# Attention values computed with the probabilities as the stationary operand, and normalised before they are turned

## The reference

```python
s = einsum('bqhd,bkhd->bhqk', q, k) * 64 ** -0.5 + bias      # causal, dilated, selected or decayed
p = softmax(s, axis=-1)
o = einsum('bhqk,bkhd->bqhd', p, v)                           # then concatenated, @ w_out
```

## Time and profile before

| | before |
|---|---|
| median of 3 runs | 2513.5 us (2513.25 to 2513.96) |
| the profiled execution | 2513.96 us |
| its span | 2512.2 us |
| TensorE busy | 2414.5 us, 96% |
| VectorE busy | 1071.5 us, 43% |
| ScalarE busy | 952.6 us, 38% |
| GpSimd busy | 1006.1 us, 40% |
| mean granted TensorE clock | 0.983 |

### The profile page before, as it was taken

How to read it: one execution, slowest core, us unless ns; L and a number is a source line. 1 busy time by engine, 2 the same in 40 slices (tenths; PEclk the granted TensorE clock), 3 DMA queues, 4 the chain that set the end, 5 groups by cost and what they waited for, 6 DMA issues and landing times.

```text
span 2512.2 us, 29431 instructions
## 1 busy us (share of the span) xinstructions
PE 2414.5 (96%) x11844; PEld 1936.9 (77%) x11844; DVE 1071.5 (43%) x1947; ACT 952.6 (38%) x1322; POOL 1006.1 (40%) x789
## 2 busy tenths in 40 slices
PE   7999999999999989999999988999999998999997
PEld 6777588888877766888888757888888867888886
DVE  4677541221347765221226465422225757422224
ACT  5345352332443444322335444422223484422222
POOL 4423054444443232444445413344444333444442
PEclk9999999999999999999999989999999999999998
DMA  4212022322232121322322211233322312223331
GB/s 150 84 51 93 17 85 100 101 92 93 83 103 84 51 76 34 101 91 94 101 101 97 84 34 51 84 101 101 97 89 84 118 50 77 88 89 101 101 101 51
DMA packets 138279, 212.36 MB, mean 85 GB/s; under 512 B 7456, under 2 KB 65952, under 8 KB 137888
## 3 DMA queue, kind: packets, MB, share of 16 engines
q1 hardware_dynamic: 138144, 210.48, 25.9%
HBM read 208.36 MB, written 2.10 MB: 84 GB/s over the span
## 4 chain that ended last, share of the span: by engine, by line
PE 54%; DVE 5%; ACT 2%; issue 2%; POOL 1%; POOLq 0%; DVEq 0%; ACTq 0%
PE ps L306 45%; PE ps L331 4%; DVE x L653 1%; POOL w_lo L269 1%; PE ps L1696 1%; PE ps L468 1%; PE ps L771 1%; PE ps L752 1%; PE ps L792 1%; DVE h_lo L543 0%; DVE tmp_both L648 0%; ACT w_hi L260 0%; PE ps L1191 0%; PE ps L1199 0%; DVE p_more L457 0%
## 5 line engine op out<-in xcount | busy, mean ns | idle before, releaser
L269 POOL TENSOR_TENSOR w_lo<-raw,w_hi 128x512 fp32r<-128x512 f32 (+1 forms) x776 | 995.6, 1315 | 1470.0 <-ACT w_hi L260 1470.0
L306 PE MATMUL ps<-h_hi,w_hi 128*128 128x512 f32 x1696 | 681.1, 402 | 12.7 <-POOL w_lo L269 10.8
L306 PE MATMUL ps<-h_hi,w_lo 128*128 128x512 f32 x1696 | 662.8, 391 | 0.0
L306 PE MATMUL ps<-h_lo,w_hi 128*128 128x512 f32 x1696 | 662.7, 391 | 0.0
L260 ACT ACTIVATE w_hi<-raw 128x2048 fp32r<-128x2048 f32 (+2 forms) x196 | 363.4, 1855 | 743.4 <-PE ps L306 725.0
L306 PE MATMUL ps<-hid_hi,w_hi 128*128 128x512 f32 x992 | 390.4, 394 | 5.0 <-DVE hid_lo L861 3.9
L306 PEld LDWEIGHTS ps<-h_hi,w_hi 128*128 128x128 f32 x1696 | 319.4, 188 | 88.7 <-issue 21.3
L306 PE MATMUL ps<-hid_hi,w_lo 128*128 128x512 f32 x992 | 387.2, 390 | 0.0
L306 PE MATMUL ps<-hid_lo,w_hi 128*128 128x512 f32 x992 | 387.0, 390 | 0.0
L306 PEld LDWEIGHTS ps<-h_lo,w_hi 128*128 128x128 f32 x1696 | 319.3, 188 | 69.1 <-issue 5.8
L306 PEld LDWEIGHTS ps<-h_hi,w_lo 128*128 128x128 f32 x1696 | 318.8, 188 | 68.9 <-issue 0.6
(11 more groups left out here) (292 smaller groups left out, 2810.1 us busy)
## 6 DMA issues: line engine op xcount, KB each, us to landing
raw<-in_w_up SPq DMA_DIRECT2D x32, 1024.0 KB, 5.2
raw<-in_w_down SPq DMA_DIRECT2D x32, 1024.0 KB, 5.0
raw<-in_ffn_w_gate SPq DMA_DIRECT2D x44, 512.0 KB, 4.0
raw<-in_ffn_w_up SPq DMA_DIRECT2D x44, 512.0 KB, 5.0
raw<-in_w_in SPq DMA_DIRECT2D x20, 1024.0 KB, 5.0
raw<-in_ffn_w_down SPq DMA_DIRECT2D x20, 1024.0 KB, 5.1
raw<-in_w_out SPq DMA_DIRECT2D x8, 1024.0 KB, 5.1
raw<-in_ev_w_in SPq DMA_DIRECT2D x8, 1024.0 KB, 5.3
```

Of the source, the lines that this page charges most:

```text
L269: pool.tensor_tensor(w_lo[r][:, k, 0:slot.width], raw[r][:, k, 0:slot.width], w_hi[r][:, k, 0:slot.width].bitcast(F32), ALU.subtract).then ...
L306: mm = pe.matmul(o, lh, rh, start=first and q == 0, stop=last and q == 2, skip_group_check=True)
```

## The change

`values` runs for one unit at a time, with the turned probabilities (128 columns) stationary and the values (64 columns) moving. The result is token-major, one head beside the other, in bank 3. VectorE inverts the row sums and multiplies them in by broadcast, from bank 3 into `on` (in the place of `rb`). TensorE turns the normalised result in `back`, four transposes into bank 2, and the high and the low part are made from there. `rb`, its turning and its copy are gone. The order in TensorE's step becomes scores, turn, beside, values, back, and VectorE's product moves to the step 4 behind the last unit, high and low part to the step 6 behind it.

```diff
@@ values, turn_sums
+            def values(self, pe, i):
+                j, qb, e = self.units[i]
+                h, c = 2 * j + e, (2 * qb + e) * HD
+                pe.wait_ge(*at("pT_copied", self.u0 + i + 1))
+                if i % 8 == 0 and j >= 1:
+                    pe.wait_ge(*at("o_norm", self.b0 + j))
                 for kb in range(qb + 1):
-                    for e in range(2):
-                        h = 2 * j + e
-                        mm = pe.matmul(ps[HD * e:HD * e + HD, 3, qb * P:(qb + 1) * P],
-                                       self.v[:, kb, h * HD:(h + 1) * HD], pT[(i + e) % self.TS][:, kb, :],
-                                       start=kb == 0, stop=kb == qb, skip_group_check=True)
+                    mm = pe.matmul(ps[:, 3, c:c + HD], pT[i % self.TS][:, kb, :],
+                                   self.v[:, kb, h * HD:(h + 1) * HD], start=kb == 0, stop=kb == qb,
+                                   skip_group_check=True)
                 sg["pv_done"].by(mm)
+
+            def back(self, pe, j, turned):
+                pe.wait_ge(*at("o_norm", self.b0 + j + 1))
+                pe.wait_ge(*at("pT_copied", self.u0 + turned))
+                for qb in range(TB):
+                    mm = pe.transpose(ps[:, 2, qb * P:(qb + 1) * P],
+                                      on[:, 2 * qb:2 * qb + 2, :].rearrange("p a b -> p (a b)"), ident)
+                sg["oT_ready"].by(mm)
+                self.backs += 1
@@ turn
-                if self.turned:
-                    pe.wait_ge(*at("rb_copied", self.b0 + self.turned))
+                if self.backs:
+                    pe.wait_ge(*at("mix_lo", self.b0 + self.backs))
@@ tensor
-                    u = i - self.VAL - 1
-                    if 0 <= u < n and u % 2 == 0:
-                        self.values(pe, u)
-                    j = self.at_end(i, self.TURN_SUMS)
-                    if j is not None:
-                        self.turn_sums(pe, j)
-                        beside(i)
                     if self.TURN <= i < n + self.TURN:
                         self.turn(pe, i - self.TURN)
-                    if j is None:
-                        beside(i)
+                    beside(i)
+                    if self.VAL <= i < n + self.VAL:
+                        self.values(pe, i - self.VAL)
+                    j = self.at_end(i, self.VAL + 2)
+                    if j is not None:
+                        self.back(pe, j, min(n, i - self.TURN + 1))
@@ vector
-                    j = self.at_end(i, self.SUMS)
+                    j = self.at_end(i, self.VAL)
                     if j is not None:
-                        dve.wait_ge(*at("p_ready", self.u0 + 8 * j + 8))
-                        link(dve, dve.reciprocal(sr[:, 8 * j:8 * j + 8], sd[:, 8 * j:8 * j + 8]))
-                        if self.b0 + j:
-                            dve.wait_ge(*at("o_norm", self.b0 + j))
-                        sg["sr_ready"].by(dve.tensor_copy(
-                            rb[:].rearrange("p (h d) -> p h d", d=HD),
-                            sr[:, 8 * j:8 * j + 8].unsqueeze(2).to_broadcast([P, 8, HD])))
-                    j = self.at_end(i, self.OUT)
-                    if j is not None:
-                        dve.wait_ge(*at("rb_copied", self.b0 + j + 1))
-                        dve.wait_ge(*at("pv_done", (self.u0 + 8 * j + 8) // 2))
-                        sg["o_norm"].by(dve.tensor_tensor(self.key[:, self.mix0 + j, :], ps[:, 3, :], rb[:], ALU.mult))
-                    j = self.at_end(i, self.LOW)
+                        dve.wait_ge(*at("pv_done", self.u0 + 8 * j + 8))
+                        if j >= 1:
+                            dve.wait_ge(*at("oT_ready", self.b0 + j))
+                        a0, a1 = 8 * j, 8 * j + 8
+                        link(dve, dve.reciprocal(sr[:, a0:a1], sd[:, a0:a1]))
+                        sg["o_norm"].by(dve.tensor_tensor(
+                            on[:], ps[:, 3, :].rearrange("p (h d) -> p h d", d=HD),
+                            sr[:, a0:a1].unsqueeze(2).to_broadcast([P, 8, HD]), ALU.mult))
+                    j = self.at_end(i, self.VAL + 2)
                     if j is not None:
                         dve.wait_ge(*at("mix_hi", self.b0 + j + 1))
                         b = self.mix0 + j
-                        sg["mix_lo"].by(dve.tensor_tensor(hid_lo[:, b, :], self.key[:, b, :],
-                                                          hid_hi[:, b, :].bitcast(F32), ALU.subtract))
+                        sg["mix_lo"].by(dve.tensor_tensor(hid_lo[:, b, :], ps[:, 2, :], hid_hi[:, b, :].bitcast(F32),
+                                                          ALU.subtract))
@@ scalar
-                    j = self.at_end(i, self.TURN_SUMS)
-                    if j is not None:
-                        act.wait_ge(*at("rb_ready", self.b0 + j + 1))
-                        sg["rb_copied"].by(act.activation(rb[:], ps[:, 2, :], ACT.Copy))
...
-                            act.wait_ge(*at("pv_done", (u - self.TS) // 2 + 1))
+                            act.wait_ge(*at("pv_done", u - self.TS + 1))
...
-                    j = self.at_end(i, self.HIGH)
+                    j = self.at_end(i, self.VAL + 2)
                     if j is not None:
-                        act.wait_ge(*at("o_norm", self.b0 + j + 1))
-                        sg["mix_hi"].by(act.activation(hid_hi[:, self.mix0 + j, :], self.key[:, self.mix0 + j, :],
-                                                       ACT.Copy))
+                        act.wait_ge(*at("oT_ready", self.b0 + j + 1))
+                        sg["mix_hi"].by(act.activation(hid_hi[:, self.mix0 + j, :], ps[:, 2, :], ACT.Copy))
```

More of the change, by code:

```diff
@@ L148, in build @@
         stat = place("stat", [P, 4 * P])
-        rb = place("rb", [P, S], where=t_off["rs2"])
+        on = place("on", [P, 8, HD], where=t_off["rs2"])
         colT = place("colT", [P, TB * IDX_H + 2 * TB])
@@ L171, in build @@
             "pool_hi pool_lo gn_in gn_mean gn_c gn_sq gn_var gn_rstd gn_out ret_hi ret_lo mix_hi mix_lo s_ready "
-            "s_masked nmax p_ready pT_ready pT_copied pv_done sr_ready rb_ready rb_copied o_norm post xup wf_split x_final stored "
+            "s_masked nmax p_ready pT_ready pT_copied pv_done o_norm oT_ready post xup wf_split x_final stored "
             "f_mm f_in f_c f_done pool_in pool_mm pool_out bias_ready conv_done xi_done root_done lru_mm lru_r lru_t "
@@ L734, in build, with __init__ @@
             TURN, VAL = 2, 4
-            SUMS, TURN_SUMS, OUT, HIGH, LOW = 2, 3, 5, 6, 7
-            def __init__(self, heads, q_hi, q_lo, val, key, bias, mix0, u0, b0, decay=None):
-                self.q_hi, self.q_lo, self.v, self.key, self.bias = q_hi, q_lo, val, key, bias
+            def __init__(self, heads, q_hi, q_lo, val, bias, mix0, u0, b0, decay=None):
+                self.q_hi, self.q_lo, self.v, self.bias = q_hi, q_lo, val, bias
                 self.mix0, self.u0, self.b0, self.decay = mix0, u0, b0, decay
@@ L773, in turn @@
                 sg["pT_ready"].by(mm)
[L775 to L781, removed]
             def values(self, pe, i):
-                j, qb, _ = self.units[i]
-                pe.wait_ge(*at("pT_copied", self.u0 + i + 2))
-                if i % 8 == 0 and self.b0 + j:
+                j, qb, e = self.units[i]
+                h, c = 2 * j + e, (2 * qb + e) * HD
+                pe.wait_ge(*at("pT_copied", self.u0 + i + 1))
+                if i % 8 == 0 and j >= 1:
                     pe.wait_ge(*at("o_norm", self.b0 + j))
                 for kb in range(qb + 1):
-                    for e in range(2):
-                        h = 2 * j + e
-                        mm = pe.matmul(ps[HD * e:HD * e + HD, 3, qb * P:(qb + 1) * P],
-                                       self.v[:, kb, h * HD:(h + 1) * HD], pT[(i + e) % self.TS][:, kb, :],
-                                       start=kb == 0, stop=kb == qb, skip_group_check=True)
-                sg["pv_done"].by(mm)
+                    mm = pe.matmul(ps[:, 3, c:c + HD], pT[i % self.TS][:, kb, :],
+                                   self.v[:, kb, h * HD:(h + 1) * HD], start=kb == 0, stop=kb == qb,
+                                   skip_group_check=True)
+                sg["pv_done"].by(mm)
+            def back(self, pe, j, turned):
[6 more added lines that the diff above has]
+                self.backs += 1
             def at_end(self, i, lag):
@@ L804, in tensor @@
             def tensor(self, pe, beside):
-                self.turned = 0
+                self.backs = 0
                 n = len(self.units)
@@ L1068, in first_layer @@
             s0 = pl.s0
-            dil = Attention(DIL_H, dil_q_hi, dil_q_lo, dil_v, key, logc, 4, 0, 0)
-            dsa = Attention(DSA_H, dsaq_hi, dsaq_lo, dsa_v, key,
+            dil = Attention(DIL_H, dil_q_hi, dil_q_lo, dil_v, logc, 4, 0, 0)
+            dsa = Attention(DSA_H, dsaq_hi, dsaq_lo, dsa_v,
```

(2 more changed lines are left out.)

## The result

The changed kernel takes 2578.35 us (median of 4 runs, 2570.0 to 2581.4), the kernel before 2513.4 us on the same chip (2512.5 to 2514.0): a ratio of 1.0253, with a 95% interval from 1.0229 to 1.0277. That is 65 us, where 41 were forecast and 58 was the upper end of the range. The profiled execution took 2571.64 us, its span is 2569.9 us and its mean granted clock 0.975 (before 0.983); the runs near the median have 0.974.

What follows compares the result with a forecast made beforehand. The prediction took TensorE, busy for 96% of the span, as the bound. Its terms, 34.9 - 15.1 + 1.4 + 21 + 3.8 - 7.6 + 5.0 - 2.4 = +41.0 us on 2514, gave 2555 us, range 2524 to 2572.

Steps and rivals of the forecast that it cites:

- The value matmuls: 640 value matmuls in the attentions: 0.109 us each, at the weight load's pace, instead of 0.055; +34.9 us.
- The first rival: Weight load of the value matmuls hides, 0.056 us per instruction: 2524 us; chance 0.08.
- The switches: Entries into and exits from the narrow array shape around `values` end: 4.5 + 10.6, so -15.1 us.
- The new waits: TensorE's waits at pair ends: `dil` +21, `dsa` +3.8, `fox` +5.0 us; added matmul time inside existing waits -2.4 us.
- the wait before `turn_sums`: In `dsa`, 2.38 us of idle time and the half clock behind it end: 3.8 us a layer, -7.6 us.
- first wait: `dil` pair ends, `turn` in step 8j+13 waits for ScalarE's copy: 2.4, 1.5 and 1.5 us.
- second: `dil` pair ends, `turn` in step 8j+14 waits for the low part: 0.6 us each.
- third: `dil` pair ends, `turn` in step 8j+15 waits for the exponential of unit 8j+14: 1.3, 0.9 and 1.9 us.
- The tail: Last pair of `dil`: its chain is no longer behind tiles, 0.5 us longer.
- The longest idle time: Sign in `fox`: TensorE's 6.41 us idle time should stay and come about 3 us later.
- TensorE's idle time in `dil`: Sign: it should rise from 3 to about 20 us, with three waits at each pair end.
- The second rival: New waits of `dil`, `dsa` and `fox` (29.8 us) are near zero: 2525 us; chance 0.11.

Runs made afterwards that it cites:

- run 6: Changed kernel with each unit's value matmuls issued twice, 640 instructions more and the same output: 2624.8 us, ratio 1.0452.
- run 7: Kernel before the change with each call's value matmuls issued twice in the narrow form, 640 instructions more: 2531.8 us, ratio 1.0086.
- run 11: Changed kernel with each value matmul cut into two of 32 moving columns, 640 instructions more, no streamed column more: 2653.0 us, ratio 1.0555.
- run 12: Kernel of run 9 with value matmuls cut into two of 32 moving columns, all of one half, then the other: 2602.2 us, ratio 1.0364.
- run 4: Kernel before the change with each call of `values` in two parts around `turn`, 48 more entries and exits of the narrow shape: 2527.3 us, ratio 1.0063.
- run 9: Changed kernel with the filler matmuls of Run 2 and VectorE's product behind its `beside` of the same step: 2532.7 us, ratio 1.0075.
- run 5: Kernel of run 3 with the filler matmuls of Run 2: 2494.1 us, ratio 0.9931 against the kernel before the change.
- run 3: Kernel before the change with `turn_sums` of the last pair of `dsa` one step later: 2504.5 us, ratio 0.9972.
- Run 2: Changed kernel with dummy matmuls of 512 columns, whose results nobody reads, in TensorE's idle time in `dsa` and `fox`: 2557.3 us, ratio 1.0181.

## Why the prediction was wrong

The direction and the causes named were right; the size was not, and the error is in the clock. Some terms were right only in sum.

**The value matmuls: right.** 0.109 us forecast, 0.111 measured, 0.114 in run 6; the narrow form 0.055 in run 7. Runs 11 and 12 show that the streamed columns don't set the pace. The weight load of 190 ns is what is left: the transposes of the earlier trace rows, with 128 stationary columns too but with the quicker loads, start 0.07 us apart. No run varied the load alone, so a fixed cost of this form of instruction isn't excluded. The first rival (an instruction at 0.056 us) is out either way. The Trainium skill, "TensorE: Matmul & The Clock Gate", section "Back-to-back issue gap", says of its formula, which the prediction weighed, that it holds for an isolated matmul, and that in a stream of loads and matmuls both set the spacing, with 81 ns at 128 columns. The trace agrees that the streamed columns don't count alone, but the number here is 111 ns at 64 and at 32 columns, two instructions of float32 to a product.

**The switches: right**, 0.30 us measured for a pair of them against 0.27 to 0.28 taken (run 4). Matmuls and switches together: runs 9 and 5 have the same fillers and little half clock. The five stretches are 523.5 us long in the one and 487.6 in the other; of these 35.9 us, idle time is 11.8 (37.1 against 25.3), half clock 10.2 x 0.46 = 4.7, and work the rest, 19.4 us. Forecast was 34.9 - 15.1 + 1.4 = 21.2. The sum is measured, its two parts only by their price per piece.

**The new waits: right in sum.** In the profiled execution TensorE's idle time rose by 17.5 us in `dil` and 4.8 in `fox` and fell by 1.9 in `dsa`, +20.4 us. The forecast's waits are 21 + 3.8 + 5.0 - 2.4, less 2 x 2.38 for the wait before `turn_sums` that went: +22.6. One by one, in `dil`: first wait 3.1, 1.3 and 1.4 (forecast 2.4, 1.5, 1.5), second 0.6 each (0.6), third 0.9, 0.6 and, in the second layer, 1.5 (1.3, 0.9, 1.9). The wait before `turn_sums` is gone, without one of its size at `back`. The tail was taken too small: 0.5 us more was forecast. The wait for the low part behind the last pair grew from 1.95 to 2.56 us, and one of 1.07 us before `back` came with it, 1.7 us more. In `fox` the sum is luck in part. The longest idle time, which was to stay and come 3 us later, fell from 6.41 to 5.42 us and came 5 us later, and there are new waits of 3.29 us before `turn` and of 1.58 us before `back`. Among its signs the prediction let TensorE's idle time in `dil` rise from 3 to about 20 us; the 3 are of one layer and the rise of 21 is for both. Measured is 9.2 to 26.7 us for both. The second rival is out.

The right total of `dil` is luck too. By runs 9 and 5, which have no half clock there, its two layers have 7.7 us more work where about 10 were forecast, and idle time rose by 17.5 us where 21 were forecast. Half clock, which the forecast didn't have there, made up the difference: 30.1 - 7.7 - 17.5 = 4.9 us for 10.2 us of it.

**The clock: the step that failed.** "Against that goes the wait of 2.38 us before `turn_sums` ..., together with the half clock ... that follows", -7.6 us. As a term it was sized well (run 3: 4.2 us a layer). But it was the only place where the sum had the clock in it. Every new wait was priced at its own length, with nothing for the half clock behind it, and the half clock behind the waits that were there before was taken to stay. The five stretches had 41.0 us of half clock before and 85.3 after, +44.4 us, which at 0.46 us lost per us is 20.4 us. Of the 44.4 us, 17.1 stand behind the old wait of 2.18 us in the first `dsa`; the rest is the balance behind waits that are new or changed, against those that ended. With it the execution closes: 20.4 idle, 20.4 clock and 19.4 work are 60.2 us, against 59.5 measured in the five stretches (1.9 of which the start gave back). The price is measured in `dsa` and agrees in `dil`. In `fox` it is less certain: from run 3 to run 5 its half clock fell by 10.2 us and the stretch by 2.0 us only, about 0.2 us per us; at that price the clock term would be 3.5 us less. Run 2 brought the half clock back to the 41.0 us of the kernel before and gave 2557 us, 2 us from the forecast.

The median is 6.7 us above the profiled execution. The runs near it have a clock of 0.974 instead of 0.975, which is 4 to 9 us more half clock and, as an estimate, 2 to 4 us of time. Where these microseconds stand in those executions isn't recorded.

No bound of the forecast took this in. The earlier trace rows showed a matmul at half speed behind one wait and the windows of the earlier trace rows a clock of 0.94 and 0.92, so the price of half clock could have been read; I charged none to waits of 1.3 to 3.1 us. The length could not have been read: behind the wait of 2.18 us it was 6.8 us in both layers.

What stays open is what sets the length of a half clock. In the attention stretches of both kernels it begins behind a wait each time, but behind the same wait of 2.18 us in `dsa` it lasted 23.9 us in one layer and 6.8 in the other, of one execution of one kernel, in run 3 6.8 and 17.1, and in run 11 10.2 and 64.9. So it isn't shown either that the change is what made it 23.9 us there; run 3, whose `values` are those of the kernel before, reached 17.1. Over whole executions the change does lower the clock: it is 0.972 to 0.977 in all five of the kernel after and 0.982 to 0.986 in those of the kernel before. Why retention's stretch in `dsa` and the pooling stretch in `fox` hold TensorE at 1.2 GHz longer than `dil` (3.4 to 6.8 us at a time) was not tried.

## What to carry to other kernels

Price a matmul by the larger of its two sides: with 128 x 128 float32 stationary blocks it was 0.111 us at 64 and at 32 moving columns, the side of the load. Turning the operands round (64 stationary, two halves of the array beside each other) is worth 0.055 us each, against 0.30 us for entering and leaving the narrow shape. With 10 instructions a call, the mean here, that pays; with 4 (0.22 us) it wouldn't, as an estimate from the two prices. A wait that VectorE has to stand out belongs behind the operations that others need sooner: this one move gave 25 us here. And a wait on the busiest engine costs its length plus the half clock behind it, which can differ between two layers of one execution, so look at the clock behind old waits too; a few matmuls that nobody reads, in the wait itself, took that part back (21 us after the change, 10 us in the kernel before).

## What the runs showed of the hardware that wasn't expected

The half clock can outlast by far the wait it stands behind: 23.9 and 27.3 us after the change, 64 us in run 11, TensorE being busy throughout in the first and the last. It costs 0.46 us per us of it in `dsa`. Its length differs between two identical layers and so between runs, which may be where the 11 us between the fastest and the slowest run after the change come from (2570.0 us at a clock of 0.977, 2581.4 at 0.972: some 26 us more half clock, 12 us at 0.46, as an estimate); in run 5, with 6.8 us of half clock in the attentions, five runs lie within 3.3 us. The first interval in a row of value matmuls is that of the stream, 0.06 us at 64 columns and 0.03 at 32, and all others are 0.111: as if one load were ready beforehand and none after it.
